# mLSTM head loop: state products and block products of a head put into two groups, transposes ahead of the maximum rows, scores last

## The reference, cut to what matters

```python
def step(state, inp):                     # one chunk of tokens
    C, n, m = state
    b = jnp.cumsum(fc, axis=-1)
    logw = jnp.where(lower, b[..., :, None] - b[..., None, :] + ic[..., None, :], -jnp.inf)
    log_inter = b + m[..., None]
    m_t = jnp.maximum(log_inter, jnp.max(logw, axis=-1))
    w_inter = jnp.exp(log_inter - m_t)
    s = jnp.einsum('bhtd,bhsd->bhts', qc, kc) * jnp.exp(logw - m_t[..., None])
    num = w_inter[..., None] * jnp.einsum('bhvd,bhtd->bhtv', C, qc) + jnp.einsum('bhts,bhsv->bhtv', s, vc)
    den = w_inter * jnp.einsum('bhd,bhtd->bht', n, qc) + jnp.sum(s, axis=-1)
    h = num / jnp.maximum(jnp.abs(den), jnp.exp(-m_t))[..., None]
    return mlstm_state_update(state, kc, vc, ic, b), h
...
    h = rmsnorm(hf + rev(hb), out_g)      # per head
    return jnp.dot(h * jax.nn.sigmoid(o), w_out)
```

## Time and profile before

| | |
|---|---|
| Time, median of 3 runs (lowest, highest) | 2902.92 us (2902.1, 2913.47) |
| The profiled execution: its own time, its span | 2902.85 us, 2901.0 us |
| PE busy | 2635.5 us, 91% of the span |
| PE weight loads busy | 2032.7 us, 70% |
| DVE, ACT, POOL busy | 1297.1, 932.1, 173.3 us |
| Mean granted TensorE clock | 0.946 |
| The head loop, from the first state product to the last transposes | from 1549.3 to 1639.0 us |

### The profile page before, as it was taken

One profiled execution on the slowest core, in us unless ns is written; L12 is line 12 of the kernel. 1 busy time (PEld: TensorE's weight loads), 2 busy tenths in 40 slices (PEclk: granted clock), 3 DMA queues, 4 the chain that ended last, 5 costly groups with the idle time before them and its releaser, 6 DMA issues.

```text
span 2901.0 us, 35381 instructions
## 1 busy us (share of the span) xinstructions
PE 2635.5 (91%) x14496; PEld 2032.7 (70%) x14496; DVE 1297.1 (45%) x2324; ACT 932.1 (32%) x1619; POOL 173.3 (6%) x134
## 2 busy tenths in 40 slices
PE   4988799997999999989998989999979989949997
PEld 2765555585888888867876667777858866828765
DVE  3235378835333333354435453334452264373463
ACT  3234355623212122234233332222332143332342
POOL 0000001001101011010000010101100001000010
PEclk9999889997999999998999899999979999969898
DMA  5123300011343332211120135553211210102201
GB/s 213 64 70 92 119 13 1 1 44 59 114 132 110 123 118 68 68 55 59 59 73 1 30 121 169 167 171 127 88 55 62 60 54 1 54 23 84 98 1 58
DMA packets 66001, 223.20 MB, mean 77 GB/s; under 512 B 7216, under 2 KB 10928, under 8 KB 65072
## 3 DMA queue, kind: packets, MB, share of 16 engines
q1 hardware_dynamic: 63648, 214.13, 22.9%
q10 hardware_dynamic: 2192, 6.82, 0.6%
HBM read 218.82 MB, written 2.10 MB: 76 GB/s over the span
## 4 chain that ended last, share of the span: by engine, by line
PE 82%; DVE 10%; ACT 4%; DMA 2%; issue 1%; POOL 0%; SPq 0%; DVEq 0%; ACTq 0%
PE pair L959 21%; PE pair L961 20%; PE pair L960 20%; PE pair L1069 4%; DVE T L1790 3%; PE side L934 2%; PE side L1133 2%; PE pair L982 2%; ACT T L1448 2%; PE pair L1120 1%; DMA RAW<-in_w 1%; PE pair L1002 1%; DVE HL L1782 1%; PE pair L653 1%; PE pair L652 1%
## 5 line engine op out<-in xcount | busy, mean ns | idle before, releaser
L959 PE MATMUL pair<-HH,WH 128*128 128x512 f32 (+1 forms) x2432 | 886.5, 365 | 70.2 <-DVE HL L1782 67.5
L961 PE MATMUL pair<-HH,WL 128*128 128x512 f32 (+1 forms) x2432 | 865.6, 356 | 0.0
L960 PE MATMUL pair<-HL,WH 128*128 128x512 f32 (+1 forms) x2432 | 865.3, 356 | 0.0
L959 PEld LDWEIGHTS pair<-HH,WH 128*128 128x128 f32 x2432 | 465.3, 191 | 192.8 <-DVE HL L1782 87.9
L1558 DVE TENSOR_TENSOR WL<-RAW,WH 128x1024 fp32r<-128x1024 f32 (+4 forms) x286 | 320.7, 1121 | 513.0 <-ACT WH L1224 500.4
L961 PEld LDWEIGHTS pair<-HH,WL 128*128 128x128 f32 x2432 | 466.6, 192 | 65.8
L960 PEld LDWEIGHTS pair<-HL,WH 128*128 128x128 f32 x2432 | 467.3, 192 | 62.1 <-issue 2.6
L1224 ACT CAST WH<-RAW 128x1024 fp32r<-128x1024 f32 (+4 forms) x286 | 270.3, 945 | 548.9 <-DMA RAW<-in_w 531.6
L959 PE MATMUL pair<-DH,WH 128*128 128x512 f32 (+3 forms) x624 | 232.8, 373 | 8.4 <-POOL DL L1977 4.3
L960 PE MATMUL pair<-DL,WH 128*128 128x512 f32 (+3 forms) x624 | 223.6, 358 | 0.0
L961 PE MATMUL pair<-DH,WL 128*128 128x512 f32 (+3 forms) x624 | 223.1, 358 | 0.0
(11 more groups left out here) (278 smaller groups left out, 2754.1 us busy)
## 6 DMA issues: line engine op xcount, KB each, us to landing
RAW<-in_w SPq DMA_DIRECT2D x345, 512.0 KB, 3.6
RAW<-in_w SPq DMA_DIRECT2D x49, 384.0 KB, 3.1
RAW<-in_w SPq DMA_DIRECT2D x16, 256.0 KB, 2.7
DFL<-in_dft_lat ACTq DMA_DIRECT2D x4, 1024.0 KB, 7.7
X<-in_x SPq DMA_DIRECT2D x1, 3072.0 KB, 16.4
out_x<-X SPq DMA_DIRECT2D x8, 256.0 KB, 2.0
RAW<-in_w SPq DMA_DIRECT2D x12, 128.0 KB, 2.0
RAW<-in_w SPq DMA_DIRECT2D x8, 144.0 KB, 2.1
```

The costliest lines, as they stand in the source:

```text
L959: mm(out[0:j.m, c:e], wh[k], a, start=k == 0, stop=False)
L960: mm(out[0:j.m, c:e], wh[k], b, start=False, stop=False)
L961: ins = mm(out[0:j.m, c:e], wl[k], a, start=False, stop=k == j.k - 1)
```

## The change

In `outs(h)` the loop that had a state product and a block product in turn becomes two loops: all eight state products of the head (both directions), then all eight block products, with the wait for `weighed` now ahead of the block products only. Only the first matmul into each bank of PSUM carries `start`; the others first write to places not yet written since then. The number of matmuls is the same.

In the loop over heads PE's order becomes outs(h), turn(h-1), negmax(h+2), scores(h+2), where it was outs(h), negmax(h+2), scores(h+2), turn(h-1).

```diff
         def outs(h):
...
             for d in range(2):
+                for j in range(4):
+                    mm(out_psum(d, j), QA[a:a + 64, i, d, j * P:j * P + P], CST[a:a + 64, i, j, d, :], start=j == 0 or (d, j) == (0, 3), stop=False, skip_group_check=True)
+            for d in range(2):
                 pe.wait_ge(*step("weighed", h, d))
                 for j in range(4):
-                    mm(out_psum(d, j), QA[a:a + 64, i, d, j * P:j * P + P], CST[a:a + 64, i, j, d, :], start=True, stop=False)
-                    ins = mm(out_psum(d, j), decay_tile(h, d, j), MV[:, 2 + j, h, :], start=False, stop=True)
+                    ins = mm(out_psum(d, j), decay_tile(h, d, j), MV[:, 2 + j, h, :], start=False, stop=True, skip_group_check=True)
             ins.then_inc(*pe.mark("mo", h))
...
         for h in range(HEADS):
             outs(h)
+            if h:
+                turn(h - 1)
             if h + 2 < HEADS:
                 negmax(h + 2)
                 scores(h + 2)
-            if h:
-                turn(h - 1)
         turn(HEADS - 1)
```

## The result

The changed kernel takes 2877.96 us (median of 9 runs, 2869.88 to 2891.0), the kernel before 2902.1 us (median of 9 in the same session, 2891.37 to 2913.47). The ratio is 0.991, with a 95% interval of 0.9892 to 0.9928: 0.9% faster, 21 to 31 us. A second measurement beside other kernels gave 2876.38 against 2902.41 us, ratio 0.9913 (0.9889 to 0.9938).

The account below looks back on a forecast made before the run. PE was taken to set the pace of the head loop; savings of 2.8, 16.25, 2.7 and 3.5 us (heads 0, 1 to 5, 6, 7) sum to 25.25 us off 2902.85, giving 2877 us, range 2869 to 2889.

Parts of the forecast that it names:

- A change of row count costs 0.19 us, a MATMUL 0.112: PE in the head loop: 0.19 us per switch between 64 and 128 rows, 0.112 us per MATMUL without one.
- 7.59 us without the overlap: Middle head's predicted time if state products did not run beside the last scores, against 7.28 us if they did.
- 3.40 us between two `outs`, set by `mixed`: Middle head: PE's next outs starts 3.40 us after the last, on the wait for mixed; with 3.88 us of outs, 7.28.
- DVE and ACT keep up, by 0.3 us: Middle head: DVE could start the next mix at 7.5 us after outs ends, fitting the 7.28 us period by 0.3 us.
- the move of the transposes: Head loop on PE: transposes ahead of the maximum rows delay the decays by 0.44 us but cost nothing, hidden by 0.7 us.
- The sum: Whole head loop: 2.8 (head 0), 16.25 (heads 1 to 5), 2.7 (head 6) and 3.5 us (head 7), 25.25 us less.
- Head 7: Last head, its outs after 2.79 us of PE idle: at the fallen clock 7.3 us grouped, 3.5 us less.
- Rival (c), the clock in the loop: Head loop: the clock falls to 1.2 GHz, a head costs 14.7 us, the kernel slows to 2922 us; chance 4%.
- The Trainium skill's rule on weight loads: Grouped products in outs: loads overlap matmuls only in different row groups, so starts stay near 0.21 us apart, time near 2900.
- Later stages, 3 us either way: Stages behind the head loop: clock falls come at other moments, allowed for with 3 us either way.

Follow-up runs that it names:

- all on 128 rows: Kernel before, but the state product sums over all 128 rows of QA and CST (a probe, computation changed): middle head 7.43 us instead of 10.53.
- grouping alone: Kernel before with state and block products grouped, transposes still between the scores and the next head's products: middle head 7.82 us, one whole time 2886.18 us.
- by direction: Full change, but grouped per direction: four state products, four block products, then again for the other direction; middle head 7.65 us, one whole time 2878.24 us.
- one place behind: Full change, but state and block products in turn again, each block product one place later; middle head 9.59 us, one whole time 2893.49 us.
- the order alone: Kernel before with only the head loop's new order, state and block products still in turn: middle head 9.98 us, one whole time 2903.68 us.
- split wait: Full change, but three backward state products go before the wait for mixed, the other five after: middle head 7.13 us, one execution 2876.04 us.

## Why the prediction was right

- **A change of row count costs 0.19 us, a MATMUL 0.112.** Right. `outs` is 3.87 us (3.88 predicted). The middle heads, all at the full clock, lie on two lines of the same slope:

  | order of PE | kernel | changes of row count per head | middle head, us |
  |---|---|---|---|
  | before | all on 128 rows | 2 | 7.43 |
  | before | grouping alone | 4 | 7.82 |
  | before | kernel before | 18 | 10.53 |
  | new | full change | 2 | 7.26 |
  | new | by direction | 4 | 7.65 |
  | new | one place behind | 14 | 9.59 |
  | new | the order alone | 16 | 9.98 |

  Each line gives 0.194 us per change. At equal counts the new order is 0.17 us shorter. Besides the changes it brings only this to PE, that scores and state products run side by side, so the 3.27 us per head are 16 changes, 3.10 us, and 0.17 us of overlap. The prediction's 7.59 us without the overlap was too long: two changes without it take 7.43.
- **3.40 us between two `outs`, set by `mixed`, with scores and state products side by side.** Right: 7.26 against 7.28 us for the middle head. The split wait shows that it was `mixed` that held the state products: without it they start 0.13 us earlier.
- **DVE and ACT keep up, by 0.3 us; the move of the transposes costs nothing.** Right: 0.27 us of wait ahead of `mix`, and 0.71 with the transposes moved back by one place. After the end of `outs` `low` ends at 7.18 us (7.2 predicted).
- **The sum.** Heads 0 to 6: 21.9 us by the traces (1549.26 to 1622.00 before, 72.74 us; 1553.64 to 1604.46 after, 50.82 us), 21.75 predicted. Head 7 is the mis-sized term: 7.3 predicted, 5.5 measured, because the clock fell only in its second half and came back. The gain there is 5.4, not 3.5 us. The loop gained 27.3 us, the prediction's sum 25.25, the two measured medians 24.1 and 26.0. That 2877 us met 2877.96 to 1 us is luck in part: the sum was 2 us short of the loop's gain, the first pair of medians 3.2 us, and the measurement leaves 21 to 31 us open.
- **Rival (c), the clock in the loop.** All seven stretches from head 0 on stand at 1.00.
- **The Trainium skill's rule on weight loads**, which spoke against the change (TensorE: Matmul & The Clock Gate, What overlaps and what doesn't): the runs don't bear it out for these float32 products. Sixteen loads for the same 64 rows, 188 ns each and so 3.0 us in all, go by in 1.98 us beside their matmuls.
- **Later stages, 3 us either way.** Too narrow for one execution: the stage behind the loop varies by 12 us between profiled executions of the same code, with the granted clock. The first window attention alone took about 113 us at 0.94 in two of them and 120.5 us or more at 0.83 to 0.85 in others. The medians lay 3.2 and 1.3 us below the loop's gain, about what the prediction had allowed; a single run would not have.

## What to carry to other kernels

Read the distance between matmul starts, not PE's busy time: where small float32 products that use different numbers of rows take turns, count the changes, and group the products by rows as far as PSUM's places allow, letting neighbours on opposite halves of the array follow one another. The overlap of such neighbours was worth 0.17 us a head here. Do it where PE has no wait; where PE waits for another engine, as in the window attention, an order that makes that engine's input later costs more than the changes it saves. After such a gain, look at which engine is next: here DVE had 0.27 us left per head.

## What the runs showed of the hardware

- A product of 64 rows costs the same start distance as one of 128 (0.112 us per MATMUL of 129 columns in both groups), so filling the other 64 rows costs nothing (all on 128 rows: 0.22 us for two); the change between the two does, 0.19 us.
- Products on the lower and the upper 64 rows run side by side, but the second group began 0.55 us after the first in every head of the split wait, where DVE had already read the places that they write (in the head above until 1584.37 us, with the first score at 1584.77), and 0.56 us at head 0 of the kernel before. Why not earlier is open.
- The length of the wait doesn't fix the clock's fall. After the same wait of 2.79 us head 7's `outs` took 5.4 to 5.5 us in four profiled executions whose `outs` and end of the loop are the full change's (granted clock 0.69 to 0.70), 6.8 us with grouping alone (0.54), and 4.26 us by direction (1.00). After 1.76 us, in the split wait, it took 7.1 us (0.57).
